# Expert weights loaded in 8 KB rows, gate and up in one pass, biases as three bf16 parts, and the sample rows' scatter in two column groups

## What is computed

```python
def moe(u, w_router, b_router, w_gate_up, b_gate_up, w_down, b_down):
    t = u.reshape(B * L, D)                               # 288 x 1024
    logits = (t @ w_router + b_router).astype(jnp.float32)
    vals, idx = lax.top_k(logits, TOP_K)                  # 4 of 32
    wts = jax.nn.softmax(vals, axis=-1)
    comb = jnp.einsum('tk,tke->te', wts, jax.nn.one_hot(idx, N_EXPERTS, dtype=jnp.float32)).astype(u.dtype)
    out = jnp.zeros_like(t)
    for e in range(N_EXPERTS):
        gu = t @ w_gate_up[e] + b_gate_up[e]              # w_gate_up[e]: 1024 x 2048, 8 MB
        gate = jnp.minimum(gu[:, :D_EXPERT], SWIGLU_LIMIT)
        up = jnp.clip(gu[:, D_EXPERT:], -SWIGLU_LIMIT, SWIGLU_LIMIT)
        h = (up + 1.0) * (gate * jax.nn.sigmoid(SWIGLU_ALPHA * gate))
        out = out + comb[:, e:e + 1] * (h @ w_down[e] + b_down[e])   # w_down[e]: 1024 x 1024, 4 MB
    return out.reshape(B, L, D)
```

## Time and profile before

| | |
|---|---|
| median of 3 runs | 1323.27 us |
| span of the profiled execution, first to last instruction | 1320.9 us |
| runs' median over that span | 2.4 us |
| TensorE busy | 1272.8 us, 96% of the span |
| VectorE, ScalarE, GpSimd busy | 360.9, 216.9, 28.0 us |
| expert loop on TensorE | from 286 us to 1274 us |
| bytes moved by DMA | 445.9 MB, 338 GB/s over the span |

### The profile page before, as it was taken

How to read it: one execution, slowest core, us unless ns; L and a number is a source line. 1 busy time by engine, 2 the same in 40 slices (tenths; PEclk the granted TensorE clock), 3 DMA queues, 4 the chain that set the end, 5 groups by cost and what they waited for, 6 DMA issues and landing times.

```text
span 1320.9 us, 15105 instructions
## 1 busy us (share of the span) xinstructions
PE 1272.8 (96%) x5608; PEld 548.5 (42%) x5608; DVE 360.9 (27%) x820; ACT 216.9 (16%) x403; POOL 28.0 (2%) x58
## 2 busy tenths in 40 slices
PE   5999999999999999999999999999999999999997
PEld 3777777443333333333333333333333333333342
DVE  3563002142222131322312131323131322313133
ACT  2564000150111011010101010111011010101024
POOL 1001004100000000000000000000000000000000
PEclk9999999999999999999999999999999999999998
DMA  9826335259999999999999999999999999999910
GB/s 305 303 85 219 128 128 154 76 183 407 409 409 406 411 409 410 407 410 407 409 409 407 408 404 411 408 410 404 409 409 409 405 410 408 410 403 409 410 49 36
DMA packets 127603, 445.91 MB, mean 338 GB/s; under 512 B 11046, under 2 KB 12166, under 8 KB 127544
## 3 DMA queue, kind: packets, MB, share of 16 engines
q1 hardware_dynamic: 125104, 440.31, 85.3%
q0 software_dynamic: 2368, 5.31, 1.3%
q10 hardware_dynamic: 112, 0.03, 0.0%
HBM read 444.10 MB, written 1.88 MB: 338 GB/s over the span
## 4 chain that ended last, share of the span: by engine, by line
PE 95%; ACT 3%; issue 1%; DVE 1%; DMA 0%; ACTq 0%
PE ps L807 50%; PE ps L601 18%; PE ps L797 7%; PE ps L856 7%; PE ps L782 7%; PE ps L886 2%; PE ps L790 2%; ACT gate_a L1050 1%; PE ps L593 1%; ACT poolw L1087 1%; PE ps L626 1%; PE ps L893 1%; PE ps L844 0%; PE ps L729 0%; ACT work L907 0%
## 5 line engine op out<-in xcount | busy, mean ns | idle before, releaser
L807 PE MATMUL ps<-ring,work 128*64 128x512 f32 x2048 | 450.4, 592 | 0.0
L807 PEld LDWEIGHTS ps<-ring,work 128*64 128x64 f32 x2048 | 147.2, 137 | 292.4 <-issue 292.4
L807 PE MATMUL ps<-ring,gate_a 128*64 128x512 f32 x1024 | 225.2, 592 | 0.0
L601 PE MATMUL ps<-work,ring 128*128 128x288 f32 x768 | 190.0, 409 | 0.8 <-DVE work L1156 0.7
L601 PEld LDWEIGHTS ps<-work,ring 128*128 128x128 f32 x768 | 146.6, 191 | 41.6 <-issue 1.0
L807 PEld LDWEIGHTS ps<-ring,gate_a 128*64 128x64 f32 x1024 | 73.6, 137 | 146.2 <-issue 146.2
L1461 DVE TENSOR_TENSOR u_tok<-u_tok,ps 128x512 f32<-128x512 f32 (+1 forms) x96 | 65.6, 683 | 173.5 <-PE ps L856 173.5
L856 PE MATMUL ps<-poolw 128*128 128x512 f32 x192 | 86.6, 600 | 21.5 <-ACT poolw L1087 21.5
L782 PE MATMUL ps<-x_tok,work 128*64 128x512 f32 x396 | 90.6, 592 | 0.0
L1442 DVE TENSOR_SCALAR work<-ps 128x512 f32<-128x512 f32 x32 | 22.1, 691 | 181.7 <-PE ps L807 181.7
L1077 ACT ACTIVATE work<-work 128x512 f32<-128x512 f32 x32 | 20.2, 631 | 314.0 <-DVE work L1442 314.0
(11 more groups left out here) (215 smaller groups left out, 663.1 us busy)
## 6 DMA issues: line engine op xcount, KB each, us to landing
ring<-in_w_gate_up SPq DMA_DIRECT2D x256, 1024.0 KB, 11.8
ring<-in_w_down SPq DMA_DIRECT2D x128, 1024.0 KB, 11.5
ring<-in_w_in SPq DMA_DIRECT2D x8, 2048.0 KB, 13.5
ring<-in_w_proj_b SPq DMA_DIRECT2D x2, 2048.0 KB, 7.7
ring<-in_w_proj_a SPq DMA_DIRECT2D x2, 2048.0 KB, 10.8
ring<-in_w_out SPq DMA_DIRECT2D x2, 2048.0 KB, 7.7
ring<-in_w_ple_gate SPq DMA_DIRECT2D x4, 1024.0 KB, 12.1
x_tok<-in_x_prompt SPq DMA_DIRECT2D x2, 512.0 KB, 4.0
```

Of the source, the lines that this page charges most:

```text
L601: mm = pe.matmul(out(b), lhs, rhs, start=(k == 0), stop=(k == len(pairs) - 1))
L807: mm = pe.matmul(ps[half(g), b, :], rows[:, k, :], quarter(q + k // 2)[:, k % 2, 512 * g:512 * g + 512], start=False, stop=(k == KC - 1))
```

## The change

It does five things.

1. **Pieces of 8 KB rows.** The ring's 12 MB are now 8 pieces of `w_gate_up` (128 input channels by all 2048 columns, one row of 8 KB for each partition) and 4 of `w_down` (two neighbouring rows of 4 KB, which lie together in memory, for each partition). So partition p of a down piece holds the rows 2p and 2p + 1 of 256, and the hidden rows are transposed in the same order: `h_blocks` takes every other column of `up`.
2. **Gate and up together.** Both biases are put in first, then for each of the 8 blocks gate and up are accumulated, four products for a piece, in banks 0 and 1 at once.
3. **Biases as three bf16 parts.** The table is loaded three times, into rows 0-31, 32-63 and 64-95. ScalarE rounds all 96 rows to bf16, VectorE takes the rounded values off rows 0-63, ScalarE rounds these, VectorE takes them off rows 0-31, and ScalarE rounds the rest. `pick_gu` and `pick_d` have a 1 in three rows, so the products L797 of before become bf16 products over 96 rows whose sum is the fp32 bias. The clearing of the table falls away, and `g_final` is loaded later.
4. **Where the bias steps stand.** ScalarE's three casts stand ahead of the squares of the residual, VectorE's two subtractions behind the merge of the branches and ahead of `add_out`.
5. **The scatter.** The products of the 32 sample rows are 32 columns wide instead of 128 and go to two column groups (`column_half`), and TensorE waits for both banks of a tile before it starts the tile's two products.

```diff
+GU_PIECES, PIECES = KC, KC + 4
+BIAS_PARTS = 3
+BIAS_ROWS = BIAS_PARTS * NE
...
+        pick_d = sb("pick_d", [P, CAP], BF16)
+        pick_gu = sb("pick_gu", [P, CAP], BF16)
...
+        bias_parts = flat_w[:, at:at + 3 * D // 2].bitcast(BF16)
...
+            def piece_used(q, n):
+                if q == GU_PIECES - 1 or q == PIECES - 1:
+                    chunk_filled(sp, "up" if q < GU_PIECES else "out", n - 1)
                 else:
-                    chunk_filled(sp, ["gate", "up", "out"][q // 4], n - 1)
-
-            def expert_quarter(q, e):
-                rows = bass.ds(e * D + 256 * (q % 4), 256)
-                src = gu_rows[rows, D * (q // 4):D * (q // 4) + D] if q < 8 else dn_rows[rows, :]
-                sp.dma_start(quarter(q), src.rearrange("(k p) c -> p k c", p=P)).then_inc(quarter_landed[q], 16)
-
-            for q in range(12):
+                    sp.wait_ge(piece_used_up[q], n)
+            def expert_piece(q, e):
+                if q < GU_PIECES:
+                    src = gu_rows[bass.ds(e * D + P * q, P), :]
+                else:
+                    src = dn_rows[bass.ds(e * D + 2 * P * (q - GU_PIECES), 2 * P), :] \
+                        .rearrange("(p k) c -> p (k c)", k=2)
+                sp.dma_start(whole_piece(q), src).then_inc(piece_landed[q], 16)
+            for q in range(PIECES):
                 if q % 2 == 0:
                     front_piece_used(*holder[MOE_SLOT[q // 2]])
-                expert_quarter(q, 0)
+                expert_piece(q, 0)
             with sp.Fori(1, NE) as e:
-                for q in range(12):
-                    quarter_used(q, e)
-                    expert_quarter(q, e)
+                for q in range(PIECES):
+                    piece_used(q, e)
+                    expert_piece(q, e)
...
             pool.wait_ge(state_stored, 16 * (len(stores) + 1))
+            wait_filled(pool, ("a", KC - 1))
+            for i in range(BIAS_PARTS):
+                pool.dma_start(bias[NE * i:NE * i + NE, 0:2 * D], b_gate_up[0]).then_inc(bias_landed, 16)
+                pool.dma_start(bias[NE * i:NE * i + NE, 2 * D:3 * D], b_down[0]).then_inc(bias_landed, 16)
+            for half in range(2):
+                wait_filled(pool, ("out", half, TT - 1))
             pool.dma_start(g_last, g_final.rearrange("(a d) -> a d", a=1).partition_broadcast(P)) \
                 .then_inc(g_last_landed, 16)
...
+            x_blocks = [x_rows[:, j * P:j * P + P] for j in range(4)]
+            h_pairs = up.rearrange("p (j c k) -> p j k c", j=2, k=2)
+            h_blocks = [h_pairs[:, j, k, :] for j in range(2) for k in range(2)]
...
             def begin_sums(kind, n, pick, at):
                 b = begin_chunk(pe, kind, n)
                 for g in range(2):
-                    pe.matmul(ps[half(g), b, :], pick, bias[:, at + 512 * g:at + 512 * g + 512],
+                    pe.matmul(ps[half(g), b, :], pick[0:BIAS_ROWS, :],
+                              bias_parts[0:BIAS_ROWS, at + 512 * g:at + 512 * g + 512],
                               start=True, stop=False)
...
+            def weigh_gate_up(n):
                 for k in range(KC):
-                    if k % 2 == 0:
-                        pe.wait_ge(quarter_landed[q + k // 2], n * 16 + 16)
-                    for g in range(2):
-                        mm = pe.matmul(ps[half(g), b, :], rows[:, k, :],
-                                       quarter(q + k // 2)[:, k % 2, 512 * g:512 * g + 512],
-                                       start=False, stop=(k == KC - 1))
-                    if k % 2 == 1 and k < KC - 1:
-                        mm.then_inc(quarter_used_up[q // 4][k // 2], 1)
+                    pe.wait_ge(piece_landed[k], n * 16 + 16)
+                    for kind, at in (("gate", 0), ("up", D)):
+                        b = CHUNK_BANK[kind]
+                        for g in range(2):
+                            mm = pe.matmul(ps[half(g), b, :], xg[:, k, :],
+                                           whole_piece(k)[:, at + 512 * g:at + 512 * g + 512],
+                                           start=False, stop=(k == KC - 1))
+                        if k == KC - 1:
+                            mm.then_inc(filled[b], 1)
+                    if k < KC - 1:
+                        mm.then_inc(piece_used_up[k], 1)
+            def weigh_down(n):
+                b = CHUNK_BANK["out"]
+                for j in range(KC // 2):
+                    q = GU_PIECES + j
+                    pe.wait_ge(piece_landed[q], n * 16 + 16)
+                    for i in range(2):
+                        for g in range(2):
+                            mm = pe.matmul(ps[half(g), b, :], hT[:, 2 * j + i, :],
+                                           quarter(q)[:, i, 512 * g:512 * g + 512],
+                                           start=False, stop=(2 * j + i == KC - 1))
+                    if j < KC // 2 - 1:
+                        mm.then_inc(piece_used_up[q], 1)
...
                         begin_sums("gate", n, pick_gu, 0)
+                        begin_sums("up", n, pick_gu, D)
                         chunk_read(pe, "xT", n)
-                        weigh("gate", 0, n, xg)
-                        begin_sums("up", n, pick_gu, D)
-                        weigh("up", 4, n, xg)
+                        weigh_gate_up(n)
                         gather(n + 1)
...
-                    for i in range(2 * TT):
-                        bank, turn = pair_bank(i)
-                        pe.wait_ge(emptied[bank], m * 2 + (bank_uses[bank] + turn))
-                        pe.matmul(ps[:, bank, :], sel_wT[:, i // 2, :], o_pair[:, 512 * (i % 2):512 * (i % 2) + 512],
-                                  start=True, stop=True).then_inc(filled[bank], 1)
+                    for t in range(TT):
+                        for h in range(2):
+                            bank, turn = pair_bank(2 * t + h)
+                            pe.wait_ge(emptied[bank], m * 2 + (bank_uses[bank] + turn))
+                        for h in range(2):
+                            bank, turn = pair_bank(2 * t + h)
+                            pe.matmul(ps[column_half(("y", t, h)), bank, :], sel_wT[:, t, 0:ROWS[t]],
+                                      o_pair[:, 512 * h:512 * h + 512], start=True, stop=True).then_inc(filled[bank], 1)
...
+            act.wait_ge(bias_landed, 16 * 2 * BIAS_PARTS)
+            act.wait_ge(state_stored, 16 * (4 + 3 * DB))
+            for i in range(BIAS_PARTS):
+                rows = BIAS_ROWS - NE * i
+                if i:
+                    act.wait_ge(bias_rest, i)
+                nc.scalar.copy(bias_parts[0:rows, :], bias[0:rows, :]).then_inc(bias_cast, 1)
...
+            for i in range(1, BIAS_PARTS):
+                rows = BIAS_ROWS - NE * i
+                dve.wait_ge(bias_cast, i)
+                V.tensor_tensor(bias[0:rows, :], bias[0:rows, :], bias_parts[0:rows, :], ALU.subtract) \
+                    .then_inc(bias_rest, 1)
...
+                        V.tensor_tensor(x_half, x_half, ps[column_half(("y", t, i % 2)), bank, :], ALU.add) \
+                            .then_inc(emptied[bank], 1)
```

59 lines of the change are left out of this document (26 added, 33 removed).

## The result

| | before | after |
|---|---|---|
| median | 1323.2 us (1322.92 to 1324.1, 4 runs) | 1279.28 us (1278.56 to 1279.52, 4 runs) |
| ratio, with its 95% interval | | 0.9667 (0.9653 to 0.968) |
| span of the profiled execution | 1320.9 us | 1277.7 us |
| granted TensorE clock, mean | 0.997 | 0.998 |
| 24 pieces of 1 MB, the weights of a pair, late in the loop | 61.7 us, set by TensorE | 59.64 us, set by the weights |

The change saves 43.9 us, 3.3%. The page of the kernel after begins to tell why; these are its busy times, its packets, and the chain that ended last by engine and by line.

What follows compares the result with a forecast made beforehand. The prediction took TensorE and the weights' stream as level to 0.5%, with the weights ending the loop after the change: -41.7 (loop), -0.4 (last scatter), +1.0 (bias staging) make -41 us, 1282 us; range 1276 to 1309.

## What to carry to other kernels

When two limits are level, a change to one alone shows little, here 6 and 9 us of 44: cost both for one round of the loop, ask which is next and how far, and change them together. A stream that is never idle ends at its first landing plus the other pieces times pace (here 296.4 + 371 x 2.485 = 1218.4, and 1220.1 measured, as the first two distances are 2.9 and 3.9 us), so its time is worked out from the price of a packet and the moment at which the first buffer comes free, and the engines' work only has to stay below. Where packets carry whole rows, lay neighbouring rows on one partition, as the runs up to 16 KB reward it: the order of a contraction is free if the other operand is transposed with the same stride.
